# ff stores issued by ScalarE behind its third snapshot, and a reordered change from the up to the down projection

## The reference, cut to what matters

```python
h = h + rmsnorm(mix, post_mix_gain[l])
v = rmsnorm(h, pre_mlp_gain[l])
ff = jnp.square(jax.nn.relu(jnp.einsum("bsd,df->bsf", v, mlp_w_up[l])))
ff = jnp.einsum("bsf,fd->bsd", ff, mlp_w_down[l])
h = h + rmsnorm(ff, post_mlp_gain[l])
```

## Time and profile before

| what | us |
|---|---|
| median of 3 runs | 2214.26 (2202.41 to 2214.7) |
| the profiled execution, its own time | 2210.1 |
| its span, first to last instruction | 2208.4 |
| PE busy in the span | 2123.3 |

### The profile page before, as it was taken

How to read it: one execution, slowest core, us unless ns; L and a number is a source line. 1 busy time by engine, 2 the same in 40 slices (tenths; PEclk the granted TensorE clock), 3 DMA queues, 4 the chain that set the end, 5 groups by cost and what they waited for, 6 DMA issues and landing times.

```text
span 2208.4 us, 28872 instructions
## 1 busy us (share of the span) xinstructions
PE 2123.3 (96%) x9781; PEld 1746.2 (79%) x9781; DVE 1435.3 (65%) x2309; ACT 1050.7 (48%) x1821; POOL 239.0 (11%) x228
## 2 busy tenths in 40 slices
PE   8999999999999999899999899999599999999997
PEld 6777788888888788778888788888478888888885
DVE  4876666665666547777766766665576766666666
ACT  5664545545545434555556655555133333323333
POOL 6011000000001000044200000001343300000001
PEclk9999999999999999999999999999799999999999
DMA  7245644635535726488656755555867735444467
GB/s 265 103 165 199 212 136 150 208 119 162 205 120 169 240 96 202 143 263 276 204 154 195 250 163 146 150 156 153 290 223 255 257 117 166 144 152 136 140 152 169
DMA packets 317493, 397.82 MB, mean 180 GB/s; under 512 B 15296, under 2 KB 204256, under 8 KB 317392
## 3 DMA queue, kind: packets, MB, share of 16 engines
q1 hardware_dynamic: 295728, 317.46, 45.7%
q0 software_dynamic: 19360, 70.72, 10.2%
q10 hardware_dynamic: 2304, 8.39, 0.9%
HBM read 262.09 MB, written 134.41 MB: 180 GB/s over the span
## 4 chain that ended last, share of the span: by engine, by line
PE 79%; DVE 5%; DMA 2%; ACT 2%; SPq 1%; issue 1%; ACTq 0%; DVEq 0%; POOLq 0%
PE o_ps L1848 19%; PE o_ps L1850 19%; PE o_ps L1849 19%; PE m_unit_ps L516 18%; SPq L1665 1%; DVE w_lo L2252 1%; DMA ff_d<-o_stage_c 1%; PE o_ps L1879 1%; PE m_nd_ps L577 0%; PE m_bank L565 0%; PE m_nd_ps L576 0%; PE m_s_ps L556 0%; DVE w_lo L2333 0%; PE m_nd_ps L528 0%; PE m_nd_ps L529 0%
## 5 line engine op out<-in xcount | busy, mean ns | idle before, releaser
L516 PE MATMUL m_unit_ps<-u_hi,w_hi 128*128 128x512 f32 x768 | 309.6, 403 | 1.3 <-ACT floor L796 1.0
L516 PE MATMUL m_unit_ps<-u_hi,w_lo 128*128 128x512 f32 x768 | 300.8, 392 | 0.0
L516 PE MATMUL m_unit_ps<-u_lo,w_hi 128*128 128x512 f32 x768 | 300.3, 391 | 0.0
L1848 PE MATMUL o_ps<-w_hi,o_s_hi 128*128 128x512 f32 x704 | 275.0, 391 | 8.4 <-ACT o_stage_c L2040 5.5
L2480 DVE TENSOR_TENSOR o_acc<-o_ps,o_acc 128x512 f32<-128x512 f32 x256 | 172.0, 687 | 164.0 <-PE o_ps L1850 163.6
L1850 PE MATMUL o_ps<-w_hi,o_s_lo 128*128 128x512 f32 x704 | 274.0, 389 | 0.0
L1849 PE MATMUL o_ps<-w_lo,o_s_hi 128*128 128x512 f32 x704 | 273.9, 389 | 0.0
L2072 ACT ACTIVATE o_s_hi<-o_s_lo 128x512 fp32r<-128x512 f32 x129 | 81.2, 632 | 242.1 <-DMA o_s_lo<-ff_d 241.7
L516 PEld LDWEIGHTS m_unit_ps<-u_hi,w_lo 128*128 128x128 f32 x768 | 144.9, 189 | 32.1
L516 PEld LDWEIGHTS m_unit_ps<-u_hi,w_hi 128*128 128x128 f32 x768 | 145.1, 189 | 29.7 <-issue 1.7
L516 PEld LDWEIGHTS m_unit_ps<-u_lo,w_hi 128*128 128x128 f32 x768 | 145.3, 189 | 27.6
(11 more groups left out here) (383 smaller groups left out, 4486.4 us busy)
## 6 DMA issues: line engine op xcount, KB each, us to landing
o_s_lo<-ff_d SPq DMA_DIRECT2D x129, 256.0 KB, 2.7
o_up_raw<-in_mlp_w_up SPq DMA_DIRECT2D x32, 1024.0 KB, 6.0
ff_d<-o_stage_c SPq DMA_DIRECT2D x128, 256.0 KB, 6.0
u_hi<-uhi_d SPq DMA_DIRECT2D x12, 2048.0 KB, 10.6
u_lo<-ulo_d SPq DMA_DIRECT2D x12, 2048.0 KB, 15.1
ff_d<-o_stage_s SPq DMA_DIRECT2D x96, 256.0 KB, 5.7
o_a_lo<-ff_d SPq DMA_DIRECT2D x95, 256.0 KB, 2.8
w_raw<-in_w_in POOLq DMA_DIRECT2D x24, 512.0 KB, 5.3
```

The costliest lines, as they stand in the source:

```text
L516: last = nc.tensor.matmul(unit_bank[u][:], w[u][:, c, :], x[:, b, c, :], start=(c == 0 and z == 0), stop=(c == KT - 1 and z == 2))
L1848: nc.tensor.matmul(dst, sh, mh, start=(begins and i == 0), stop=False, skip_group_check=not begins)
```

## The change

`DownOrder` lists the first four products as (a11,0), (a11,1), (s2,0), (s2,1) instead of (a11,0), (s2,0), (a11,1), (s2,1), and the first down forms s4, s3, a22 and a12 are split two to seven steps later. `store_ff` leaves SP; ACT issues the seven stores of set S - 1 in set S, behind `snapshot` 2 and ahead of `next_slot` 2. In the last set `rectify`, the last `square` and the four `ff_sum` go into the down phase (ACT step 3, DVE step 4), and the stores of the last set are issued by ACT in steps 5 to 8, two a step.

```diff
-        self.products = [pu for products in sets for pu in products]
-        self.set_of = [s for s, products in enumerate(sets) for pu in products]
+        placed = sorted((max(s, 1), list(DOWN).index(p) if s < 2 else 0, s, n, (p, u))
+                        for s, products in enumerate(sets) for n, (p, u) in enumerate(products))
+        self.products = [x[-1] for x in placed]
+        self.set_of = [x[2] for x in placed]
...
-        rest = [(1, ("s4", 0)), (4, ("s3", 0)), (6, ("a22", 0)), (9, ("a12", 0))]
+        rest = [(3, ("s4", 0)), (6, ("s3", 0)), (9, ("a22", 0)), (16, ("a12", 0))]
...  SP
-            def store_ff(S, b, B):
-                sp.wait_ge(*squared.at((S + 1) * 4))
-                sp.wait_ge(*ff_sum_made.at((S + 1) * 4))
-                for i, p in enumerate(DOWN):
-                    src = stage[ff_block[p]][b][:].rearrange("p (j o t) -> p j o t", o=1, t=P)
-                    sp.dma_start(k["ff_d"][i, B][:, :, ds(S - PAIRS * B, 1), :], src).then_inc(ff_out[b].sem, 16)
...
-                if not is_set(S, 0) and not is_set(S, SETS - 1):
-                    store_ff(S - 1, 1 - b, 0 if is_set(S, PAIRS) else B)
...
-                    for n, m in ((0, 0), (2, 1), (2, 2), (3, 3)):
-                        sp.wait_ge(*up_mm.at(S * 7 + n + 1))
+                    for m in range(4):
+                        sp.wait_ge(*up_mm.at(S * 7 + m + 1))
                         load_ff(m)
                     load_down("s1", 0)
-                    sp.wait_ge(*up_mm.at(S * 7 + 5))
-                    load_down("s4", 0)
-                    store_ff(S - 1, 1 - b, B)
...
-                if m < 2:
-                    load_down(("s3", "a22")[m], 0)
-                if m == 2:
-                    store_ff(SETS - 1, 1, 1)
-                if m == 4:
-                    load_down("a12", 0)
-                if m == 6:
+                if m in (0, 1, 3, 10):
+                    load_down({0: "s4", 1: "s3", 3: "a22", 10: "a12"}[m], 0)
+                if m == 12:
...  ACT
+            def store_ff(S, b, B, part=tuple(DOWN)):
+                act.wait_ge(*squared.at((S + 1) * 4))
+                act.wait_ge(*ff_sum_made.at((S + 1) * 4))
+                for p in part:
+                    i = list(DOWN).index(p)
+                    src = stage[ff_block[p]][b][:].rearrange("p (j o t) -> p j o t", o=1, t=P)
+                    act.dma_start(k["ff_d"][i, B][:, :, ds(S - PAIRS * B, 1), :], src).then_inc(ff_out[b].sem, 16)
...
                     snapshot(S, j, b, 2)
+                    store_ff(S - 1, 1 - b, 0 if is_set(S, PAIRS) else B)
                 next_slot(S, j, b, 2)
...
-                rectify(S, j, b)
-                square(S, b, 3)
+                else:
+                    rectify(S, j, b)
+                    square(S, b, 3)
...
+                if m == 3:
+                    rectify(SETS - 1, PAIRS - 1, 1)
+                    square(SETS - 1, 1, 3)
+                if 5 <= m <= 8:
+                    store_ff(SETS - 1, 1, 1, tuple(DOWN)[2 * (m - 5):2 * (m - 4)])
...  DVE
+                if m == 4:
+                    for n in range(4):
+                        ff_sum(SETS - 1, PAIRS - 1, 1, n)
```

More of the change, by code:

```diff
@@ L2384, in up_set @@
                         ff_low(m)
[L2385 to L2388, removed]
                     down_low("s1", 0)
-                next_slot(S, j, b, 6)
-                ff_sum(S, j, b, 3)
+                else:
+                    for n in range(3):
+                        ff_sum(S, j, b, n)
+                    next_slot(S, j, b, 6)
+                    ff_sum(S, j, b, 3)
             def amid_squares(n, i):
```

## The result

The changed kernel takes 2243.53 us (median of 4 runs, 2239.01 to 2243.73); the kernel before, on the same chip, 2210.11 (4 runs, 2202.41 to 2214.7). The ratio is 1.015, with a 95% interval of 1.0113 to 1.0187: slower by 33 us, where the forecast was 2209. The profiled execution took 2243.72.

A forecast was written before the change was run, and what follows sets the result against it. PE bounds the kernel, busy 2123.3 of 2208.4 us, so only its waits or low clock can yield gains. Terms -23.5 + 14.7 + 6.5 + 1.3 = -1.0 against 2210.1 gave 2209 us, range 2188 to 2241.

The forecast's parts named there:

- Phase change, -23.5: Change from up to down: 33.5 us of waits and low clock go, 10 us of new waits come; -13.5 to -30.5.
- the first high part: Phase change: ACT issues seven stores before the down phase's high parts, costing about 0.5 us at the first product.
- none over 6: Phase change, sign in the trace after: several PE waits of about 1 us, none over 6 us.
- item (4): Phase change: ff blocks are loaded only 8.2 us ahead of use; one load took 7.47, just too late with splitting.
- item (3): Phase change: products 6 and 7 follow the split of the s4 form and four `ff_sum`, about 1 us each.
- Ordinary sets, 0.7 us: Sets 7 to 13 and 17 to 30: ACT's burst of stores makes PE wait 0.7 us a set, +14.7 us.
- Sets 1 to 6, +6.5: POOL's transfers hold ACT about 1 us more a burst: 10.2 us, less removed waits, +6.5 (0 to 15).
- The removed waits: Sets 1 to 6: two waits of 3.7 us together, from late snapshots, should go.
- The turn, +1.3: Sets 14 to 16: splitting a form costs 9.0 us, its earlier load saves 7.7; +1.3 us (-4 to +5).
- Rival A: Loop: ACT held 1.2 us at each seventh store, PE waits 1.9 us a set; 2241, slower; chance 0.22.
- The rule of the Trainium skill: Loop: all engines' DMAs share 16 DMA engines, so another issuing engine saves only sequencer time; spoke against stores on ACT.

The follow-up runs named there:

- phase_only: The changed kernel, but SP issues the stores of sets 0 to 29 again; 2188.99 us, ratio 0.9915 to the kernel before.
- all_sp: The changed kernel, but SP issues all stores of `ff_d`, with products, forms and sums in the changed order; 2192.02 us, ratio 0.992 to the kernel before.
- two_and_five: The changed kernel, but two of the seven stores go out behind the second snapshot and five behind the third; 2225.55 us, ratio 1.0075 to the kernel before.
- pool_later: The changed kernel, but POOL begins its early sums only when the fourth set's weights are made; 2237.04 us, ratio 1.0129 to the kernel before.

## Why the prediction was wrong

- **Phase change, -23.5: held.** -20.1 in the profiled execution, 20.5 to 23.6 us gained by the count of matmuls in the five kernels with this program, and -19.8 between the medians of phase_only and its kernel before (2208.76). The waits of 20.50 and 6.07 went, and the new ones came from two of the places named (the first high part, product 6): 6.95 us, or 9.5 with the slow first product, against 10 with the clock. But the one behind the burst was sized at 0.5 us and was 3.38: the error of the next points, here too. And the one at product 6 was 3.13 us in this execution but 6.1 to 7.3 in the four others with this program, so "none over 6" was luck. It is the late ff load of item (4) of the text, and the split of item (3) behind it.
- **Ordinary sets, 0.7 us: held, in part by luck.** 0.80 a set by period. The working behind it (start of the first store, spacing, the chain s2 high part, s2 low part, `join` 0, a22 low part, `join` 1) stands in the trace row by row, and one store less removes it, as a slack of about 4.5 us demands. But the spacing came from the last two of SP's seven stores in that set. All seven took 6.9 us, as the rows below show, with issues of 1.16 and 1.40 us among them. That none was held on ACT, where the burst stands 5 us behind the load of up weights and not right behind it, the text had no row for. Nor did the row at 924.39 show that ACT stands still while it issues: it names a wait for DVE. The rows of the changed kernel show it (the issue at 1159.04 ends at 1159.61, and the high part starts at 1159.73).
- **Sets 1 to 6, +6.5: the step that failed.** The text took the DMA share of 0.88 against 0.53, and from it "about 1 us more" of ACT's hold a burst. The text had no row under that 1 us. Measured: 23.4 us, 3.9 a set; issues of up to 3.37 us, a burst of 10.5. The range ended at 15. The rows were in the trace of the kernel before, on SP's queue. First the fourth and the last of the seven stores in set 1, then the first, the fourth and the last in the quiet set of the earlier trace rows:

```profile
955.84 2.86 SPq L1665 DMA_DIRECT2D ff_d<-o_stage_s  x1
...
962.49 0.89 SPq L1665 DMA_DIRECT2D ff_d<-o_stage_c  x1
...
1121.81 0.56 SPq L1665 DMA_DIRECT2D ff_d<-o_stage_c  x1
...
1124.62 1.40 SPq L1665 DMA_DIRECT2D ff_d<-o_stage_s  x1
...
1127.98 0.76 SPq L1665 DMA_DIRECT2D ff_d<-o_stage_c  x1
```

  In set 1 the seven lasted from 952.64 to 963.38, 10.7 us, and in sets 2 to 6 from 6.6 to 10.7; PE did not wait for it there. The sets of 26.6 and 24.3 us pay, besides the wait, a granted clock of 0.87 and 0.93. The removed waits were mis-sized too: between 930 and 975 us line 2040 cost PE 5.5 us before, and its successor 3.6 after, so 1.9 of 3.7 went.
- **The turn, +1.3: failed in the same way.** I charged 3.0 us a set for splitting a form and took 7.7 off for a form loaded earlier. The set that took 27.1 us before took 27.2 after. Before, ACT waited 6.43 us there for the form to land; after, it did not wait for the form, but its issues held it until 1268.73, and PE waited 4.68. So the old cause went, as the text says, and the burst took its place. The set ahead of it went from 19.0 to 28.1: its burst begins 2.3 us behind SP's requests for two forms, and took 8.8 us. +11.1.
- **Rival A** named the right time, 2241, by the wrong distribution: 1.9 us in each of 30 sets. The ordinary sets paid 0.8 and the nine others 3.8 on average, the worst 9.1. I set its row of 1.84 us aside because the loop shows 0.76 at the seventh place, which is right for that place and not for the third and fourth. (Six of the seven issues of the earlier trace rows lie between 0.56 and 0.68 us, not 0.64 and 0.67.) The question to ask was what the seven issues take in each set, one by one.
- **The rule of the Trainium skill** (DMA: Bandwidth & Descriptors, section Issuing engines are not separate DMA queues) spoke against the stores on ACT, and so it came: the gain is there without ACT's queue (all_sp, 0.992), and ACT's time was spent.

## What to carry to other kernels

A DMA issue is work of the engine that issues it, with a length that depends on the other transfers: list every issue of the same transfer in the kernel before, stretch by stretch, also on a queue for which nobody waits, and price the new place by whole bursts of the stretch in question, not by two rows of a quiet one. The DMA share alone does not tell which issue is held. On an engine with deadlines put one or two issues into each pause in place of seven into one, or leave them to an engine that nobody waits for. And when a change has an ordering part and a queue part, build the ordering part alone first: here it was the whole gain (0.9915 against 1.015).

## What was not expected of the hardware

- The same issue of 256 KB took 0.55 to 0.57 us in a set with a DMA share of 0.85 and up to 4.33 us where the share was 1. In the burst at the turn the first four took 0.56 to 0.82 us, the last of them at a share of 1.03, and the fifth 4.33. What sets the place of the held one is open: in two_and_five it was the fourth of set 1 (3.31 us).
- A wait costs more than itself: behind the 6.44 us at 1248.05 the granted clock was 0.80 for 13 us, 2.6 us more; behind the 4.68 at 1274.41 it was 0.79 for 14.4 us, and behind the 3.38 at 1602.69 it was 0.50 for 5.3.
- DVE's instruction of 128x512 took 1.7 to 1.8 us beside POOL's sums, and 0.69 without (set 0 of the kernel before and of pool_later). In the changed kernel all 15 instructions of DVE of this shape that took over 1 us between 930 and 1560 us lie beside a sum of POOL.
